# A one-core encoder layer in fp32: first tiles split by halves between the value weights, products of ones ahead of them, and the routing sums, tables and first two gathers in another order

## The chip, the cores and the metric

One of the cores of a Trainium2 chip runs the whole program; the other cores are idle. The time is that of one execution on the device, in microseconds (us). The kernel before takes 1265.24 us, the median of three runs (1263.52 to 1265.70). TensorE is called PE in the rows, VectorE DVE, ScalarE ACT, GpSimd POOL and SyncE SP; SP, ACT and POOL also issue transfers (DMAs).

## The reference, cut to what matters

Two requests (512 and 1024 tokens, 1536 together, 1024 features) go through one post-norm encoder layer with shared weights. Cut to its skeleton:

```python
proj = x @ w_in                        # queries, keys and values of two head groups
oa = windowed attention (+-128 tokens) with sinks and ALiBi
ob = dilated attention, three (window, dilation) branches merged by their denominators
x1 = LN(alpha * x + concat(rms(oa), rms(ob)) @ w_out)
scores = sigmoid(x1 @ w_router)        # 16 experts in 4 groups
# best group by the sum of its two best biased scores, then top 2 inside it
y = sum over the two experts of gate * (silu(x1 @ w_gate[e]) * (x1 @ w_up[e])) @ w_down[e]
shared = (silu(x1 @ ws_gate) * (x1 @ ws_up)) @ ws_down
out = LN(alpha * x1 + y + shared)
```

All values are fp32. The kernel makes each large product of three: every operand is split in a high part (ScalarE rounds it to the matmul type) and a low part (VectorE subtracts the high part from the original), and TensorE adds high by high, high by low and low by high.

## The kernel before, in words

Each engine has its own program, written out by hand in the order of its work; semaphores (`S[...]`) hold one engine until another has counted up. Nothing but this order and these waits schedules the work. The stages that the change touches:

**Value projection (the head, functions `xt`, `vpart`, `vproj`, lines 848 to 890).** SyncE loads token tile 0 into `xin` (L512), the identity (L513), tile 1 (L514) and then, for each of the 8 slices k of the input features, 512 and 128 columns of value weights into `raw_v` (L516, L517). TensorE waits for the identity, transposes tile 0 and tile 1 (8 transposes each, L852; the first eight lie in banks 0 and 1, the others in 2 and 3), ScalarE copies the high parts into `xT`, VectorE subtracts for the low parts (L1637). Only then do both go on to the value weights: `wv_hi` on ScalarE, `wv_lo` on VectorE (L1658), one slice after another. TensorE runs, for each k, the six products of tile 0 and the six of tile 1 (L858 to L860). Tiles 2 to 11 follow one by one, the transposes of tile t+1 ahead of the products of tile t. Meanwhile SyncE stores finished value tiles (`store_v`), loads the next token tile (`load_x`), and at t == 4 issues `load_small` (constants, router weights, sinks and gains, seven small transfers). GpSimd carries the rows of `w_out` through SBUF to a scratch copy in DRAM in split form (`wo_st` counts these stores).

**First keys and queries (`PRE` projections, `dup`).** Six projections of 24 products each (512 columns) go through one pair of stage buffers: ScalarE copies the high part (`proj_high`), VectorE the low part (`proj_low`), SyncE copies stage to `KA`, `KB` or `Q` (`dup`, L579, L583), and ScalarE may fill the stage again only when that copy has landed. Ahead of the first `dup` SyncE waits for all stores of `w_out` (`wo_st`, 32 * KD). After the five first copies it loads the next weights and writes zeros to the accumulator; the sixth copy opens `pair(0)`. In `pair` TensorE interleaves 72 attention units with projections.

**Shared expert and routing (`d_step`, `dgu`, `ddn`, `dxt`, lines 1045 to 1240).** A step works on 256 tokens: `dxt` transposes them, `dgu` makes 96 products with gate and up weights in four blocks f (0 and 1 are gate, 2 and 3 up), ScalarE takes Silu, VectorE multiplies by the up half (`gated`) and takes the low part (`h_low`), `ddn` makes 12 products with the down weights for each half of the tokens, and VectorE adds them to `base` (`add_shared`). The shared expert runs on the first three tiles (n = 0, 1, 2; `EARLY` is 3), then steps of 224 slots with routed experts follow, then three late steps of the shared expert. In VectorE's program the routing stands between: `route_scores` and `route_groups` (sigmoid, ranks, the mask `msk`), then TensorE's prefix sums over tokens (L1215, L1219, in bank 2, after `d_step(1)`), `route_slots` (the place of each token in its expert's run, about 35 small operations), three `route_tables(n)` (0/1 matrices `oneA` and `oneB`, all on VectorE), TensorE's `table(n)` (8 products each, L1205, between the `ddn` calls), and `route_done` (token ids, gates and destinations by slot). Its last instruction counts `table_ready`. GpSimd then copies two columns of ids (L2256), gathers the rows of slot tile 3 into `xg` (two indirect transfers, L2261), and TensorE transposes them. The gather of tile 4 waits until those transposes are done, since it writes the same `xg`.

**Expert weights.** SyncE loads gate and up weights of the next slot tile into `raw_gu` in two halves as soon as VectorE has split the half before (`wg_lo`), and the down weights into `raw_d` (`wd_lo`). The first of these loads waits for `ej_ready`, the list of experts from `route_slots`.

## Time and profile before

| | before |
|---|---|
| median of 3 runs | 1265.24 us |
| the profiled execution's own time | 1265.37 us |
| its span, first to last instruction | 1263.5 us |
| TensorE busy | 1204.5 us (95%) |
| VectorE busy | 734.5 us (58%) |
| ScalarE busy | 578.9 us (46%) |
| GpSimd busy | 214.5 us (17%) |
| mean granted TensorE clock | 0.98 |
| transfers, mean over the span | 188 GB/s |

The profile is of one execution. "Busy" counts the time in which an engine has an instruction at work; a wait of TensorE shows as idle time, and the row that ends it names what it waited for. The granted clock is 1.0 at the full of its two levels (2.4 GHz) and 0.5 at the lower (1.2 GHz). The span is 1.9 us shorter than the execution's own time.

### The profile page before, as it was taken

What the parts mean: (1) busy time and instruction counts of PE and PEld (TensorE: products, weight loads), DVE (VectorE), ACT (ScalarE), POOL (GpSimd) and SP (SyncE); (2) the same over time, 40 slices, a digit from 0 to 9 for tenths busy, and PEclk for the clock granted to TensorE, in tenths of its full rate; (3) what the DMA queues carried; (4) which work ended last, traced back from release to release, by engine and by line L of the source; (5) the groups of instructions that cost most, each with busy time, mean ns of one, the idle gap of its engine ahead of it and who ended that gap; (6) DMA issues with size and microseconds to landing.
All of it is one profiled execution on the core that took longest, in us unless ns stands there. A gap on an engine that the chain in (4) does not pass through costs nothing.

```text
span 1263.5 us, 22065 instructions
## 1 busy us (share of the span) xinstructions
PE 1204.5 (95%) x8031; PEld 1083.0 (86%) x8031; DVE 734.5 (58%) x1790; ACT 578.9 (46%) x1416; POOL 214.5 (17%) x276
## 2 busy tenths in 40 slices
PE   6999999999999999999799999998799999999993
PEld 6998788888888888888688888897799999999892
DVE  3222355655565556555767886458566656665378
ACT  3232244544454355434443343220466766666455
POOL 1021001200120012002211112000213333333222
PEclk9999999999999999999999999899899999999997
DMA  8697664356436543748763333532899999999783
GB/s 242 204 296 252 150 168 97 93 143 147 97 77 173 117 114 80 186 132 255 205 213 137 143 118 116 189 112 67 281 302 268 284 295 274 267 282 299 189 310 143
DMA packets 162802, 237.47 MB, mean 188 GB/s; under 512 B 41328, under 2 KB 111216, under 8 KB 162672
## 3 DMA queue, kind: packets, MB, share of 16 engines
q1 hardware_dynamic: 148400, 185.00, 48.8%
q0 software_dynamic: 11776, 41.95, 13.6%
q10 hardware_dynamic: 2544, 9.44, 1.9%
q8 instruction: 50, 0.82, 0.3%
q14 instruction: 32, 0.26, 0.1%
HBM read 147.44 MB, written 59.02 MB: 163 GB/s over the span
## 4 chain that ended last, share of the span: by engine, by line
PE 82%; issue 6%; DVE 4%; DMA 3%; ACT 2%; SPq 1%; POOL 1%; DVEq 1%; ACTq 0%; POOLq 0%
PE bank L858 18%; PE bank L860 18%; PE bank L859 18%; PE bank L959 9%; PE bank L852 5%; PE bank L946 5%; PE bank L937 4%; PE bank L938 3%; PE bank L1081 2%; SPq L579 1%; SPq L583 1%; DMA a_work<-in_x 1%; POOL Q L2211 1%; DMA wo_scratch<-a_work 1%; DMA d_work<-x_scratch,idc 1%
## 5 line engine op out<-in xcount | busy, mean ns | idle before, releaser
L1345 ACT ACTIVATE b_work<-b_work 128x256 f32<-128x256 f32 (+3 forms) x288 | 148.1, 514 | 235.3 <-DVE b_work L1691 235.2
L858 PE MATMUL bank<-xgT_hi,w_gu_hi 128*128 128x224 f32 (+1 forms) x704 | 197.5, 281 | 4.4 <-ACT d_work L1571 2.3
L859 PE MATMUL bank<-xgT_lo,w_gu_hi 128*128 128x224 f32 (+1 forms) x704 | 196.2, 279 | 0.0
L860 PE MATMUL bank<-xgT_hi,w_gu_lo 128*128 128x224 f32 (+1 forms) x704 | 196.1, 279 | 0.0
L1700 DVE COPY b_work<-bank 128x256 f32<-128x256 f32 (+2 forms) x256 | 112.8, 440 | 117.3 <-PE bank L946 116.3
L858 PEld LDWEIGHTS bank<-xgT_hi,w_gu_hi 128*128 128x128 f32 x704 | 136.6, 194 | 6.6 <-issue 3.1
L859 PEld LDWEIGHTS bank<-xgT_lo,w_gu_hi 128*128 128x128 f32 x704 | 136.7, 194 | 0.7
L860 PEld LDWEIGHTS bank<-xgT_hi,w_gu_lo 128*128 128x128 f32 x704 | 136.6, 194 | 0.0
L2211 POOL CAST Q<-Q 128x512 fp32r<-128x512 f32 x48 | 53.5, 1148 | 437.8 <-DVE w_k_lo L1645 232.0
L946 PE MATMUL bank<-keep,b_work 128*128 128x128 f32 x608 | 114.8, 275 | 7.0 <-ACT b_work L1345 6.8
L946 PEld LDWEIGHTS bank<-keep,b_work 128*128 128x128 f32 x608 | 79.8, 139 | 40.2 <-ACT b_work L1345 11.8
L959 PE MATMUL bank<-b_work 128*128 128x64 f32 (+1 forms) x704 | 107.4, 268 | 0.0
L959 PEld LDWEIGHTS bank<-b_work 128*128 128x128 f32 (+1 forms) x704 | 97.1, 193 | 7.5 <-issue 2.2
L1691 DVE CUSTOM_DVE_ANT_0 b_work<-bank,tB 128x256 f32<-128x256 f32 (+2 forms) x192 | 74.8, 390 | 44.3 <-PE bank L938 40.0
L1746 DVE TENSOR_TENSOR xgT_lo<-bank,xgT_hi 128x512 fp32r<-128x512 f32 (+1 forms) x88 | 52.3, 638 | 78.1 <-ACT xgT_hi L1253 78.1
L1455 ACT ACTIVATE w_gu_hi<-raw_gu 128x512 fp32r<-128x512 f32 (+1 forms) x144 | 77.6, 622 | 33.4 <-DVE c_work L1778 22.9
L1874 DVE TENSOR_TENSOR w_gu_lo<-raw_gu,w_gu_hi 128x512 fp32r<-128x512 f32 x136 | 83.3, 682 | 0.0
L858 PE MATMUL bank<-w_o,oT_hi 128*128 128x512 f32 x192 | 76.5, 398 | 1.8 <-DVE c_work L1760 1.2
L858 PE MATMUL bank<-xT,w_q_hi 128*128 128x512 f32 x192 | 77.2, 402 | 0.0
L1253 ACT ACTIVATE xgT_hi<-bank 128x512 fp32r<-128x512 f32 (+1 forms) x88 | 44.4, 558 | 71.4 <-PE bank L852 64.4
L860 PE MATMUL bank<-xT,w_q_lo 128*128 128x512 f32 x192 | 75.6, 394 | 0.0
L859 PE MATMUL bank<-xT,w_q_hi 128*128 128x512 f32 x192 | 75.4, 393 | 0.0
(214 smaller groups left out, 2835.5 us busy)
## 6 DMA issues: line engine op xcount, KB each, us to landing
raw_gu<-in_w_gate SPq DMA_DIRECT2D x32, 512.0 KB
raw_gu<-in_w_up SPq DMA_DIRECT2D x32, 512.0 KB
raw_d<-in_w_down SPq DMA_DIRECT2D x16, 1024.0 KB, 9.5
Q<-stage_hi SPq DMA_DIRECT2D x96, 128.0 KB, 2.4
Q<-stage_lo SPq DMA_DIRECT2D x96, 128.0 KB, 2.4
o_scratch<-b_work SPq DMA_DIRECT2D x36, 264.0 KB, 3.4
c_work<-o_scratch SPq DMA_DIRECT2D x12, 792.0 KB, 5.1
wo_scratch<-a_work POOLq DMA_DIRECT2D x16, 512.0 KB, 4.0
```

Of the source, the lines that this page charges most:

```text
L852: last = nc.tensor.transpose(banks[c // 4][:, P * (c % 4):P * (c % 4) + rows], src[0:rows, P * c:P * c + P], ident[0:rows, 0:rows])
L858: nc.tensor.matmul(o, w_hi, x_hi, start=first, stop=False)
L859: nc.tensor.matmul(o, w_hi, x_lo, start=False, stop=False)
L860: return nc.tensor.matmul(o, w_lo, x_hi, start=False, stop=last)
L946: end = nc.tensor.transpose(bank[2 + u % 2][0:r, P * c:P * c + P], prob[:, u % 2, at[c]:at[c] + r], ident)
L959: end = nc.tensor.matmul(o, probT[0:r, u % 2, P * c:P * c + P], rows, start=c == 0, stop=c == len(v) - 1)
L1345: nc.scalar.activation(prob[:, u % 2, 0:n], prob[:, u % 2, 0:n], ACT.Exp, scale=-1.0, bias=o[:, HD:HD + 1], accum_out=o[:, HD + 1:HD + 2])\
L1455: nc.scalar.activation(w[0][:, bass.ds(k * 512, 512)], raw_gu.rearrange("p k f -> p (k f)") [:, bass.ds(k * 512, 512)], ACT.Copy).then_inc ...
L1691: V.tensor_tensor_reduce(out=prob[:, u % 2, 0:n], in0=bank[u % 2][:, 0:n], in1=tab, scale=-(HD ** -0.5), scalar=BIG, op0=ALU.add, op1=ALU.min,
L1700: last = V.tensor_copy(probT[:, u % 2, 0:n], bank[2 + u % 2][:, 0:n])
L1874: V.tensor_tensor(w_lo[:, w], flat[:, w], plain(w_hi[:, w]), ALU.subtract)\
L2211: end = G.tensor_copy(to.rearrange("c (r s) -> c r s", r=4), plain(slot[:, half, part, :]).rearrange("c (s r) -> c r s", r=4))
```

## The change

In the head: SyncE loads the identity first, tile 0 second, and tile 1 behind the first slice of value weights. TensorE makes six products of ones into bank 7 before it waits for the identity. Tiles 0 and 1 are transposed with a count after each four (`xt_half`), and ScalarE and VectorE take their four quarters between the slices 0 and 1 of the value weights. The transposes of tile 2 go behind slice 5. The gains are loaded ahead of `load_x(4)`, the other small constants at t == 5, and SyncE's wait for `wo_st` moves from the first `dup` into `pair(0)`.

In the routing: VectorE takes `route_scores` ahead of `gated(0)`, `route_groups` behind it; the prefix sums go into `dgu(1)` behind block 2, in bank 7; the transposes of tile 2 go behind its blocks 0 and 1; both `ddn(0)` halves follow `dgu(1)`. In `route_slots` the expert list is cut out (`route_experts`, now after the first table), and the sums of the mask by score are woven in. `oneA` is made on ScalarE (`rows_hit`). The three `table(n)` stand in `dgu(2)` behind blocks 1 and 2 and after it. `route_done` makes the ids first and counts `id_ready`; GpSimd gathers tiles 3 and 4 at once, by the table's own columns, into `xg` and `slab`. The first expert's weights are split in two parts around `add_shared(1, 1, 1)`.

```diff
# SyncE
+            sp.dma_start(ident, const[:, 0:P]).then_inc(S["id_loaded"], 16)
             sp.dma_start(xin[:, 0, :], x_t[0]).then_inc(x_ld[0], 16)
-            sp.dma_start(ident, const[:, 0:P]).then_inc(S["id_loaded"], 16)
-            sp.dma_start(xin[:, 1, :], x_t[1]).then_inc(x_ld[1], 16)
             for k in range(KD):
+                if k == 1:
+                    sp.dma_start(xin[:, 1, :], x_t[1]).then_inc(x_ld[1], 16)
...
             load_w(KA0, KA0 + HD)
+            load_gains()
+            load_x(4)
             for t in range(4, TILES):
                 store_v(t - 4)
-                load_x(t)
-                if t == 4:
+                if t > 4:
+                    load_x(t)
+                if t == 5:
                     load_small()
...
-            sp.wait_ge(S["wo_st"], 32 * KD)
             for n in range(PRE - 1):
                 what, g = FIRST[n]
                 dup(n, what, g, g, KA)
...
+                if i == 0:
+                    sp.wait_ge(S["wo_st"], 32 * KD)
                 load_v1(i)
# TensorE, head
+            pe.wait_ge(S["ones_ready"], 1)
+            for c in range(6):
+                nc.tensor.matmul(bank[7][:, 0:P], ones, ones, start=True, stop=True)
             pe.wait_ge(S["id_loaded"], 16)
...
+            def xt_first(t):
+                pe.wait_ge(x_ld[t], 16)
+                for c in range(KD):
+                    made = nc.tensor.transpose(bank[2 * t + c // 4][:, P * (c % 4):P * (c % 4) + P],
+                                               xin[:, t, P * c:P * c + P], ident)
+                    if c % 4 == 3:
+                        made.then_inc(S["xt_made" if c > 4 else "xt_half"], 1)
...
-            xt(0)
-            xt(1)
-            pe.wait_ge(S["xts_ready"], 2)
+            xt_first(0)
+            xt_first(1)
             for k in range(KD):
                 pe.wait_ge(S["wv_made"], k + 1)
                 for t in range(2):
+                    if k == 0:
+                        pe.wait_ge(S["xts_half"], t + 1)
+                    if k == KD // 2:
+                        pe.wait_ge(S["xts_ready"], t + 1)
...
-            xt(2)
+                if k == 5:
+                    xt(2)
# ScalarE and VectorE, head (VectorE alike, with wv_low)
+            xt_part(0, 0)
+            wv_high(0)
+            xt_part(0, 1)
+            xt_part(1, 0)
+            wv_high(1)
+            xt_part(1, 1)
+            for k in range(2, KD):
+                wv_high(k)
+            xt(2)
# TensorE, routing
+            def second(f):
+                if f < 2:
+                    dxt(slab, f, 2, 2)
+                if f == 2:
+                    prefix_sums()
+
+            def third(f):
+                if f in (1, 2):
+                    table(f - 1)
+
+            dgu(1, 1, 1, second)
             pe.wait_ge(S["xg_lo"], 2 * EARLY)
...
-            dgu(2, 0, 2)
+            ddn(0, 0, 0, 0)
+            pe.wait_ge(S["cum_read"], 1)
+            ddn(0, 0, 1, 0)
+            dgu(2, 0, 2, third)
+            table(2)
             ddn(1, 1, 0, 1)
-            table(0)
             ddn(1, 1, 1, 1)
-            table(1)
-            table(2)
             ddn(2, 0, 0, 2)
-            ddn(2, 0, 1, 2)
             dxt(xg, 0, EARLY, EARLY)
             dxt(xg, 1, EARLY, EARLY)
+            ddn(2, 0, 1, 2)
# ScalarE, routing, at the head of d_step(2)
+            def rows_hit(n):
+                act.wait_ge(S["rq_ready"], 1)
+                if n == 2:
+                    act.wait_ge(S["idm_made"], 1)
+                a = oneA[:, n % 2].rearrange("p c a -> p (c a)")
+                for c in range(THIRD):
+                    nc.scalar.activation(a[:, P * c:P * c + P], iota_p, ACT.Square, scale=-1.0,
+                                         bias=rq[:, 0, THIRD * n + c:THIRD * n + c + 1])
+                act.drain()
+                nc.scalar.activation(a, plain(a), ACT.Relu, scale=-1.0, bias=1.0).then_inc(S["oneA_made"], 1)
# VectorE, routing, its order
+            route_scores()
             gated(0, 0, 0)
+            route_groups()
+            xg_low(2, 0, 2)
+            xg_low(2, 1, 2, bank[5:7])
             h_low(0, 0, 0)
-            route_scores()
-            route_groups()
+            route_slots()
             gated(1, 1, 1)
-            xg_low(2, 0, 2)
+            route_tables(0)
+            route_experts()
+            route_tables(1)
+            route_tables(2)
             h_low(1, 1, 1)
-            xg_low(2, 1, 2)
             add_shared(0, 0, 0)
-            route_slots()
-            route_tables(0)
+            route_done()
+            gated(2, 0, 2)
             add_shared(0, 0, 1)
-            gated(2, 0, 2)
-            route_tables(1)
             h_low(2, 0, 2)
-            route_tables(2)
             add_shared(1, 1, 0)
-            route_done()
+            gu_split(EARLY, 1, EARLY, range(0, 4))
             add_shared(1, 1, 1)
-            gu_split(EARLY, 1, EARLY)
+            gu_split(EARLY, 1, EARLY, range(4, KD))
+            xg_low(EARLY, 0, EARLY)
+            xg_low(EARLY, 1, EARLY, bank[0:2])
             add_shared(2, 2, 0)
             add_shared(2, 2, 1)
# GpSimd
+            def first_gathers():
+                pool.wait_ge(S["xgT_made"], 2 * EARLY)
+                pool.wait_ge(S["id_ready"], 1)
+                for n, (place, sems) in enumerate(((xg, ("g_first", "g_ld")), (slab, ("g_second", "g_second")))):
+                    for h in range(2):
+                        rows, c = half_rows(EARLY, h), 2 * n + h
+                        G.indirect_dma_start(out=place[0:rows, h, :], out_offset=None, in_=x1_d,
+                                             in_offset=bass.IndirectOffsetOnAxis(ap=idtab[0:rows, c:c + 1].bitcast(U32),
+                                                                                 axis=0)).then_inc(S[sems[h]], 16)
...
-            gather(EARLY)
-            gather(EARLY + 1)
+            first_gathers()
+            pool.wait_ge(S["table_ready"], 1)
             weights(EARLY)
             gather(EARLY + 2)
```

The sources and waits that follow from this are changed with it: step 3 takes tile 4 from `slab`, `y_rows` of step 3 waits until `slab` has been transposed, and the next gather (tile 5) waits only for the transposes of tile 3.

## Rows read from the trace of the kernel before

**Rows 1.** Profile page, busy time of TensorE: us, share of the span, instructions.

```profile
PE 1204.5 (95%) x8031; PEld 1083.0 (86%) x8031; DVE 734.5 (58%) x1790; ACT 578.9 (46%) x1416; POOL 214.5 (17%) x276
```

**Rows 2.** Stretches: us, busy (instructions) of PE, PEld, DVE, ACT, POOL; clock, DMA share, GB/s.

```profile
4.61:8.30 3.69, 3.67 (x16) 3.16 (x16) 0.57 (x1) 1.09 (x2) 0.00 (x0) 1.00 1.04 374
14.87:27.39 12.52, 12.52 (x86) 12.52 (x85) 1.73 (x3) 0.69 (x3) 3.36 (x6) 0.99 0.79 175
833.87:868.00 34.13, 34.13 (x260) 32.76 (x261) 25.34 (x84) 4.20 (x8) 0.00 (x0) 1.00 0.18 60
868.00:898.76 30.76, 19.95 (x88) 16.21 (x86) 24.46 (x44) 8.54 (x17) 4.28 (x5) 0.78 0.40 123
892.30:902.50 10.20, 6.98 (x33) 6.69 (x34) 6.01 (x11) 6.11 (x12) 2.73 (x4) 0.50 1.02 344
914.00:932.00 18.00, 18.00 (x138) 16.52 (x139) 11.75 (x20) 10.96 (x21) 1.57 (x3) 1.00 0.98 347
```

**Rows 3.** Timeline of the head: start, us, engine, line, instruction, [idle before <- releaser].

```profile
1.15 0.42 SPq L513 DMA_DIRECT2D keep<-in_const  x1
10.64 5.96 DVE L1658 TENSOR_TENSOR w_v_lo<-a_work,w_v_hi 128x640 fp32r<-128x640 f32 x8
11.60 0.59 PE L858 MATMUL bank<-w_v_hi,xT 128*128 128x384 f32 x1 [3.32 <-DVE w_v_lo L1658]
30.92 0.44 PE L858 MATMUL bank<-w_v_hi,xT 128*128 128x384 f32 x1 [1.62 <-DVE xT L1637]
46.63 1.09 PE L852 MATMUL bank<-keep,a_work 128*128 128x128 f32 x8 [0.48 <-DMA a_work<-in_x]
```

**Rows 4.** Timeline of the first keys and queries, 116 to 163 us.

```profile
116.01 0.60 ACT L1253 ACTIVATE stage_hi<-bank 128x512 fp32r<-128x512 f32 x1 [4.62 <-PE bank L860]
120.20 0.52 SPq L579 DMA_DIRECT2D KA<-stage_hi  x1
144.47 0.35 PE L937 MATMUL bank<-KA,Q 128*128 128x256 f32 x1 [1.00 <-DMA Q<-stage_lo]
153.40 0.60 ACT L1253 ACTIVATE stage_hi<-bank 128x512 fp32r<-128x512 f32 x1 [2.40 <-issue]
160.87 0.60 ACT L1253 ACTIVATE stage_hi<-bank 128x512 fp32r<-128x512 f32 x1 [2.67 <-DMA KB<-stage_lo]
163.04 0.33 PE L946 MATMUL bank<-keep,b_work 128*128 128x128 f32 x1 [1.87 <-ACT b_work L1345]
```

**Rows 5.** Timeline of the routing on all engines, 835 to 894 us.

```profile
835.77 0.16 DVE L1965 COPY r_work<-keep 128x24 f32<-128x24 f32 x1
845.38 0.36 DVE L1985 SCALAR_TENSOR_TENSOR r_work<-r_work 128x192 f32<-128x192 f32 x1
856.22 0.28 DVE L2002 TENSOR_TENSOR r_work<-bank,r_work 128x112 f32<-128x112 f32 x1 [2.41 <-PE bank L1219]
865.18 0.19 DVE L2060 CAST r_work<-rq_i 128x48 f32<-128x48 int32 x1
880.21 2.01 PE L1205 MATMUL bank<-oneB,oneA 128*128 128x180 f32 x8 [3.23 <-DVE oneB L2084]
884.33 1.59 POOL L2261 DMA_INDIRECT d_work<-x_scratch,idc  x1 [0.92 <-POOL idc L2256]
893.37 3.25 PE L852 MATMUL bank<-keep,d_work 128*128 128x128 f32 x16 [4.02 <-DMA d_work<-x_scratch,idc]
```

**Rows 6.** What the moved comparison costs: VectorE's group, and ScalarE's scaled and plain copies.

```profile
L2080 DVE TENSOR_TENSOR oneA<-r_work,keep 128x1024 fp32r<-128x1024 f32 x3 | 3.7, 1219 | 0.0
46.73 0.28 ACT L1253 ACTIVATE Va<-bank 128x128 f32<-128x128 f32 x1
46.89 1.34 ACT L1296 ACTIVATE a_work<-a_work,keep 128x512 fp32r<-128x512 f32 x2
```

**Rows 7.** An expert's gate and up weights: issue of a load, and its splitting on ScalarE.

```profile
921.01 0.38 SPq L741 DMA_DIRECT2D raw_gu<-in_w_gate  x1
935.30 4.27 ACT L1455 ACTIVATE w_gu_hi<-raw_gu 128x512 fp32r<-128x512 f32 x8
```

More of the change, by code:

```diff
@@ L1044, in dxt @@
                     transposes(src[:, half, :], bank[0:2], S["xgT_made"], R1)
+                    return
+                if n == 2 and half:
+                    transposes(src[:, half, :], bank[5:7], S["xgT_made"])
                     return
@@ L1534, in d_step @@
                 soon = n in (0, EARLY, LATE0, LATE0 + 1)
+                if n == EARLY - 1:
+                    for third in range(3):
+                        rows_hit(third)
                 if EARLY <= n - 2 < LATE0 - 1:
@@ L1571, in d_step @@
                 nc.scalar.activation(hidden(sg[:, s, :], n), hidden(bank[0][:], n), ACT.Silu).then_inc(S["sg_ready"], 1)
-                if not last and not soon and n != EARLY - 1:
+                if not last and not soon and n >= EARLY:
                     xg_high(q + 1, 0, n + 1)
@@ L1579, in d_step @@
                     xg_high(q + 1, 1, n + 1, bank[0:2])
-                elif not last and not soon:
+                elif not last and not soon and n >= EARLY:
                     xg_high(q + 1, 1, n + 1)
@@ L1652, in proj_low, with xt_part, wv_low @@
                 V.tensor_tensor(lo, sums, plain(hi), ALU.subtract).then_inc(S["proj_ready"], 1)
-            xt(0)
-            xt(1)
-            for k in range(KD):
+            def xt_part(t, c):
+                dve.wait_ge(S["xs_hi" if c else "xs_half"], t + 1)
+                hi, lo = (xT[:, 0, part, 4 * c:4 * c + 4, P * t:P * t + P] for part in range(2))
+                V.tensor_tensor(lo, bank[2 * t + c][:].rearrange("p (k c) -> p k c", c=P), plain(hi), ALU.subtract)\
+                 .then_inc(S["xts_ready" if c else "xts_half"], 1)
+            def wv_low(k):
                 dve.wait_ge(S["wv_hi"], k + 1)
@@ L1659, in _ @@
                                 plain(wv_hi[:, 640 * k:640 * k + 640]), ALU.subtract).then_inc(S["wv_made"], 1)
+            xt_part(0, 0)
+            wv_low(0)
+            xt_part(0, 1)
+            xt_part(1, 0)
+            wv_low(1)
+            xt_part(1, 1)
+            for k in range(2, KD):
+                wv_low(k)
             def wo_low(k):
```

121 lines of the change are left out of this document (66 added, 55 removed).

## The prediction, made before the changed kernel ran

> **What bounds the kernel now.** The page's busy times come first: TensorE works 1204.5 us, 95% of the span [rows 1]. So only two things can shorten the time: a gap of TensorE that closes, or products at the full clock that ran at the lower one. I therefore went through TensorE's timeline stage by stage and wrote down every gap with the row that ends it; the views by stretch then give the sum and the clock. In the routing, from 868.00 to the first expert step at 898.76, TensorE is busy 19.95 of 30.76 us at a mean clock of 0.78, while the 34.13 us before are full at 1.00 [rows 2]. The largest gaps there are 3.23 us for a table of VectorE's and 4.02 us for gathered rows [rows 5]. In the head it waits 3.32 us for the value weights' low part, 1.62 us for tile 2 and 0.48 us for a tile's load [rows 3]. Around the first attention units it waits 1.00 us for a copy to Q and 1.87 us for ScalarE, which a copy to KB holds [rows 4]. In the expert steps it is full: 18.00 of 18.00 us at clock 1.00 [rows 2]. What is won ahead of them should thus stay won, if the weight stream follows.
>
> **The head, step by step.** Identity and tile 0 change places, 576 KB in both orders, and TensorE started at 4.61 when the second had landed [rows 2, 3]. I keep 4.6. The 16 first transposes took 3.67 us, 0.23 each, against 1.09 us for eight later ones, 0.13 each [rows 2, 3]: they ran at the lower clock, although the stretch's own row prints 1.00. Tile 0 costs 8 x 0.23 = 1.84 us, to 6.45. Tile 1 now stands behind 320 KB of weights, at 374 GB/s 0.9 us; it had some half us in hand, so I charge 0.4. Its transposes end at 6.85 + 1.84 = 8.7.
>
> The weights' first low part is no longer behind four quarters: half of tile 0 is transposed at 5.5, ScalarE's copy and VectorE's part take about 0.6 us each and the slice's copy and part 0.65 and 0.75 (5.96 / 8, [rows 3]), so it is made at about 7.5 to 8. The slices after it come every 0.75 us, TensorE takes 1.75 for one. Products start at 8.7 rather than 11.60. The 96 products take 96 x 12.52 / 86 = 14.0 us at full clock [rows 2]; I add 0.4 for a start at the lower one. Two sets of transposes at 0.87 net follow (tile 2 inside the loop, tile 3 after it). Tile 2's products start at 8.7 + 14.0 + 0.4 + 1.7 = 24.8 instead of 30.92 [rows 3]: **6.1**. The wait of 1.62 goes with it, since tile 2 is converted under slices 6 and 7. The 0.48 for a load goes too, as the small constants no longer stand ahead of it: **0.5**.
>
> The products of ones are an operation that the trace does not show by itself. At 0.23 each they are 1.4 us, over long before the first load lands: cost 0. If they raise the clock by 4.6, the transposes gain up to 16 x 0.10 = 1.6 us. A loss would need a later start, and nothing is behind them until 4.6. I take 0, because a pause of 2 us lies between, and keep 1.6 for the range.
>
> The first `dup` waited for the stores of w_out until 120.20, while its stage was filled at 116.01 + 0.6 + 0.7 = 117.3 [rows 4]. With that wait gone the chain of copies starts 2.9 us earlier still, and TensorE's gap of 1.00 closes: **1.0**. ScalarE's waits of 2.40 and 2.67 for the same copies shrink by about 2, so the 1.87 at 163.04 closes: **1.9**. The moved wait is harmless: SyncE reaches it some 30 us after the stores are done. Behind it stand `load_v1` and `load_v2`, first needed at unit 24. The head sums to **9.5**.
>
> **The routing, step by step.** I set one timetable, in the times of the trace before, from dgu(1) at 833.87.
>
> VectorE: scores move from 835.77 to 832.7, behind the low part of tile 1. They take 5.8 us, `gated(0)` 0.6 (to 839.1), groups 4.2 (the whole from 835.77 to 845.38 + 0.4 is 10.0 [rows 5]): the mask is ready at 843.2. TensorE: 260 products in 34.13 us are 0.13 each [rows 2], a block of 24 (256 columns) 2.9 us, eight transposes 0.87; blocks 0 to 2 with both transposes end at 844.4, so there is 1.1 in hand. The sums (3.3 us) end at 847.6. `gated(0)` would hold block 2 from 841.5; 2.4 in hand.
>
> `route_slots` took 865.18 + 0.19 - 856.22 = 9.15 us to the rows and columns [rows 5]. The expert list takes 1.3 away, the woven sums bring 0.8: 8.65, to 856.3, then 0.8 for the gates, `gated(1)` to 857.8. TensorE meanwhile has block 3 (850.6), two `ddn` of 2.9 (856.4) and dgu(2), whose table(0) stands at 862.3. VectorE's first table takes 2.5 us, to 860.3: 2 in hand.
>
> ScalarE makes `oneA` from 858.4 on. The trace has no Square of 128 columns with a pointer. The plain copy of 128 is 0.28; two scaled of 512 take 1.34, about 0.18 more than two plain ones, a pointer is 0.09; overlapped by 0.09, one is 0.28 [rows 6]. Eight are 2.25, the Relu over 1024 about 1.05, a drain 0.2: 3.5 us a third. The ends for the range are 1.22, VectorE's own price for the same 1024 columns [rows 6], and 8 x 0.67 + 1.3 = 6.7, were each as long as 512 columns. The thirds are ready at 861.9, 865.4 and 868.9, and TensorE wants them at 862.3, 866.1 and 869.9. So in hand are only 0.4, 0.7 and 1.0. The row says that ScalarE takes three times VectorE's 1.22 for this work. The Trainium skill (ScalarE: Activation LUTs, Rules for kernel authors) says the same as a rule: relu and other simple elementwise work belongs on VectorE. By the rule the comparison would stay there: VectorE's last table would be 3 x 1.14 later, at 870.7, and TensorE would wait 0.8. By the rows ScalarE is idle here (8.54 busy in 30.76 us, [rows 2]), so I cost the slower engine at 0.
>
> TensorE ends the last table at 870.8 and runs ddn(1, 0), ddn(1, 1), ddn(2, 0) to 879.4. The ids are ready at 871.2. The first gather was issued at 884.33 and both had landed by 893.37, 9.0 us, with 2 MB of weights beside them [rows 5]. Now 0.9 us of id copying is gone. At 9.0 the rows of tile 3 land at 880.4 and cost 1 us; alone, perhaps 7.5 and nothing. Their transposes end at 881.0, the last ddn at 883.9, the low parts at 884.2. The first expert step starts at 884.3 instead of 898.76: **14.5**. Checked from the other side: 10.8 us of gaps plus half of some 8.5 us of busy time at the lower clock are 15.0. Then that step ran at the lower clock until 902.50, where the stretch prints 0.50 [rows 2]: half of 3.7 is **1.9**. The routing sums to **16.4**.
>
> **What follows it.** The first expert's load begins no earlier (`ej_ready` moves from 859.4 to 861.9), but the next begins only 8.4 us earlier while its use is 14.5 earlier. ScalarE's three stores of `base` (3 MB) move forward as well. In the steady part a load is issued at 921.01 and split from 935.30, 14.3 us, with the transfer engines 98% busy at 347 GB/s [rows 2, 7]. The loads of tiles 5 and 6 get about 11 us. ScalarE may run some 3 us late before its Silu is late: I charge 0, and this is the likeliest place for a loss.
>
> **The sum.** 9.5 + 16.4 = 25.9, less 0.5 for the places with under 1 us in hand: 25.4. The profiled execution took 1265.37, within 0.15 of the median 1265.24, so **1240.0**.
>
> **The rivals.** (a) The weight stream or the gathers give some back. For it: the 98% and the eleven us; against it: no expert step of before waits for a weight. 2 to 7 us: 1242 to 1247. (b) The head gives less, because tile 1 or the value weights arrive later than the even 374 GB/s says, or the lower clock lasts: products from 10.5 and 1.6 more, 3.4 us: 1243.5. (c) The tables turn: ScalarE at 6.7 a third pushes the three tables by about 3, 6 and 9 us, and ids with them. 9 us: 1249. A table load between Silu and Square would cost only 1.3 once. The Trainium skill (ScalarE: Activation LUTs, Table sets) says that cheap functions such as relu stand in every set, which speaks against such a load; the trace shows no Square right behind a Silu in this stage. (d) The stream, not TensorE, sets the pace of the experts, so that they end when they did and the whole routing gain is swallowed: 1256. (e) Slower than before: the 14.3 us become the bound. ScalarE splits the weights ahead of its Silu, so a load landing late holds Silu, `gated`, the split of the hidden values and ddn in each of about 15 routed steps. It decides from 25.4 / 15 = 1.7 us a step; at 2 us a step 1265.4 - 25.4 + 30 = 1270. Against it: the steps are as long as before and ask for the same bytes, so a late start should be made up. (f) It does not do what it says: VectorE's own order costs TensorE what the table's waits cost, and only the head is left: 1256 as in (d).
>
> **How the numbers follow.** Forecast, everything within 1237 to 1242: 0.56. (a) 0.20, (b) 0.10, (c) 0.05, (d) and (f) 0.05, (e) 0.03, a gain above the forecast by the 1.6 of the ones 0.01. Low: 1240 - 1.6 - 1.4 for waits that I charged, 1237. High: through (a) and (b), 1248; beyond it lie (c) to (e), 0.13. About 0.2%, 2.5 us, is what a measurement can tell from no change. Faster: all but (e) and a remainder, 0.96; same 0.01; slower 0.03.
>
> **What would show it.** Tile 2's products at 24 to 26 us instead of 30.92; no wait for Q at the first unit and none of 1.87 behind it; from dgu(1) to the first expert step some 50.5 us with under 2 of gaps and a clock of 1.00; table products that wait for nothing or under 1 us for `oneA`; transposes of tile 3 at about 9 us behind the ids. Wrong would be: a wait for raw_gu on ScalarE with TensorE gaps behind 890, a first table behind 863, or value products that start later than 10.

## The result, and the profile after

The changed kernel took 1245.5 us (median of 4 runs, 1241.7 to 1247.8) beside 1265.5 of the kernel before: a ratio of 0.983, 95% interval 0.981 to 0.985, so it is 20 us faster. Forecast were 1240.0, with 1237 to 1248. Side and range hold; the sum was 5.5 us too good, and the result lies outside the band of 1237 to 1242 that the forecast proper gave 0.56, in that of the rivals (a) and (b). The execution profiled is the slowest of the four, 1247.77 us (span 1245.9).

The page's busy times of the changed kernel:

```profile
PE 1200.8 (96%) x8043; PEld 1079.9 (87%) x8043; DVE 730.3 (59%) x1787; ACT 589.1 (47%) x1443; POOL 217.2 (17%) x274
```

TensorE is busy for 3.7 us less than in [rows 1], with 12 more instructions, and the span is 17.6 us shorter: 13.9 us of the gain are closed gaps, the rest is busy time. The same stretches as in [rows 2] (us, busy of PE, PEld, DVE, ACT, POOL, granted clock, DMA share, GB/s), and one of the attention:

```profile
14.87:25.50 10.63, 10.63 (x77) 10.63 (x76) 2.74 (x4) 2.12 (x6) 3.35 (x6) 1.00 1.08 230
157.60:164.40 6.80, 6.45 (x23) 5.88 (x24) 3.02 (x10) 1.99 (x8) 0.00 (x0) 0.50 0.96 267
832.12:866.25 34.13, 33.98 (x261) 32.82 (x262) 28.12 (x88) 13.27 (x34) 0.00 (x0) 1.00 0.12 33
866.25:881.71 15.46, 15.46 (x88) 12.75 (x87) 14.28 (x29) 8.12 (x15) 4.43 (x4) 1.00 0.82 232
```

From the second shared block's start (832.12, before 833.87) to the first expert step (881.71, before 898.76) TensorE now runs 49.44 of 49.6 us, all at the full clock. These 49.6 were 64.9. The stretch at 157.60 ran at 0.50, the lower level; the kernel before was at 1.00 there.

The head's timeline, to be held against [rows 3]:

```profile
1.03 2.93 PE L874 MATMUL bank<-keep 128*128 128x128 f32 x12 [1.03 <-DVE keep L1705]
4.95 1.06 PE L880 MATMUL bank<-keep,a_work 128*128 128x128 f32 x8 [0.99 <-DMA a_work<-in_x]
8.08 1.97 PE L880 MATMUL bank<-keep,a_work 128*128 128x128 f32 x8 [2.07 <-DMA a_work<-in_x]
9.70 0.67 PE L866 MATMUL bank<-w_v_hi,xT 128*128 128x384 f32 x1
...
26.13 0.42 PE L866 MATMUL bank<-w_v_hi,xT 128*128 128x384 f32 x1
```

The six fp32 products of ones are 12 instructions in 2.93 us. Tile 0's eight transposes took 1.06 us, the pace of the full clock; tile 1's took 1.97 after 2.07 us of waiting for its load. Tile 2's products start at 26.13 instead of 30.92. The first keys and queries, against [rows 4]:

```profile
110.46 0.60 ACT L1298 ACTIVATE stage_hi<-bank 128x512 fp32r<-128x512 f32 x1 [4.62 <-PE bank L868]
111.81 0.51 SPq L581 DMA_DIRECT2D KA<-stage_hi  x1
119.93 0.60 ACT L1298 ACTIVATE stage_hi<-bank 128x512 fp32r<-128x512 f32 x1 [8.88 <-DMA KA<-stage_lo]
139.06 0.36 PE L962 MATMUL bank<-KA,Q 128*128 128x256 f32 x1 [0.97 <-DMA Q<-stage_lo]
155.77 0.60 ACT L1298 ACTIVATE stage_hi<-bank 128x512 fp32r<-128x512 f32 x1 [2.99 <-DMA KB<-stage_lo]
157.95 0.69 PE L971 MATMUL bank<-keep,b_work 128*128 128x128 f32 x2 [2.19 <-ACT b_work L1405]
```

The copy to KA is issued at 111.81, 8.4 us earlier than before, but ScalarE can use the stage again only at 119.93. The gaps of 1.00 and 1.87 that I expected closed are there: 0.97 and 2.19. The routing, against [rows 5, 6]:

```profile
830.09 1.28 ACT L1651 ACT_TABLE_LOAD   x1
856.61 2.44 ACT L1600 ACTIVATE oneA<-keep,r_work 128x128 fp32r<-128x128 f32 x8
859.11 1.06 ACT L1603 ACTIVATE oneA<-oneA 128x1024 fp32r<-128x1024 f32 x1
860.23 1.13 PE L1252 MATMUL bank<-oneB,oneA 128*128 128x180 f32 x8
868.92 0.22 DVE L2184 TENSOR_SCALAR idtab<-bank 128x60 int32<-128x60 f32 x1 [1.09 <-PE bank L1252]
870.06 1.10 POOL L2353 DMA_INDIRECT d_work<-x_scratch,idtab  x1 [63.78 <-DVE idtab L2184]
877.24 1.78 PE L860 MATMUL bank<-keep,d_work 128*128 128x128 f32 x16
884.47 2.19 ACT L1515 ACTIVATE w_gu_hi<-raw_gu 128x512 fp32r<-128x512 f32 x4 [4.30 <-DMA raw_gu<-in_w_up]
892.05 0.85 PE L860 MATMUL bank<-keep,slab 96*128 96x96 f32 x8 [1.17 <-DVE xgT_lo L1841]
```

A third of `oneA` takes 2.44 + 1.06 = 3.5 us; it ends at 860.17, and the table's products start at 860.23 without a wait. The gathered rows are transposed 8.1 us behind the end of the ids' row (869.14), without a wait, but with nothing in hand: in e5, whose trace has the landings, the second half lands at 874.63 and its transposes start at 874.80. One small new wait, 1.17 us, stands in the second expert step. It comes from the weights: ScalarE waits 4.30 us for a load, so VectorE's low parts of the weights and, behind them, of the rows come late. That is the sign that the prediction had named for being wrong, a wait for `raw_gu` with a gap of TensorE's behind 890.

The profiled execution, added up: 5.5 us gained by the first key projection (104.7 for 110.3), 3.8 lost again by the second shared block (832.12 for 833.87 is all that is left), 15.3 gained to the first expert step, 0.5 behind it: 17.6. Of the 3.8, 2.3 go ahead of the first shared block (787.7 for 790.9) and 1.5 between it and the second, where this stretch was at the lower clock:

```profile
806.10:816.30 10.20, 10.04 (x47) 10.08 (x48) 5.07 (x6) 3.24 (x8) 0.18 (x1) 0.50 1.01 396
```

Every profile has such a stretch there. It lasts 6.8 us in eight of them (before, e1, e2, e4 to e7, e12; 42.9 to 43.0 us from block to block) and 10.2 us in six (the first of the changed kernel, e3, e8 to e11; 44.3 to 44.5 us). The changed kernel had 10.2 in its first profile and 6.8 in e5, so this 1.5 us differs between executions of one program; whether the change makes the longer one likelier isn't shown.

### The profile page after: what moved, and what is told of

Same layout as the page of the kernel before. It is cut to its first block, busy times and chain, and to the rows that moved or that the text cites. A ratio compares the mean times of both kernels' runs of the same rounds, so it can differ in the third digit from the quotient of the medians.

```text
span 1245.9 us, 22130 instructions
## 1 busy us (share of the span) xinstructions
PE 1200.8 (96%) x8043; PEld 1079.9 (87%) x8043; DVE 730.3 (59%) x1787; ACT 589.1 (47%) x1443; POOL 217.2 (17%) x274
## 4 chain that ended last, share of the span: by engine, by line
PE 75%; issue 10%; DVE 4%; DMA 3%; ACT 2%; POOL 2%; SPq 2%; ACTq 1%; POOLq 0%; DVEq 0%
PE bank L866 17%; PE bank L868 16%; PE bank L867 16%; PE bank L984 9%; PE bank L971 5%; PE bank L860 4%; PE bank L962 4%; PE bank L963 3%; SPq L585 1%; POOL c_work L2278 1%; PE bank L1114 1%; DMA KA<-stage_lo 1%; DVE c_work L1873 1%; SPq L581 1%; DVE c_work L1871 1%
## 5 line engine op out<-in xcount | busy, mean ns | idle before, releaser
L868 PE MATMUL bank<-w_o,oT_lo 128*128 128x512 f32 x192 | 74.9, 390 | 0.0
```

The lines of the kernel that those rows point to most:

```text
L868: return nc.tensor.matmul(o, w_lo, x_hi, start=False, stop=last)
```

## The experiments

Each was timed in five rounds beside the kernel before; "gain" is one less the ratio, with its 95% interval, in us of 1266. Times of different jobs are compared by these ratios.

**One half at a time.** The head's edits alone (e1), then the routing's alone (e2).

> The kernel before with the head's half of the change alone. My theory after reading the changed kernel's profile: the head brings 5.5 us by the start of the first key projection (104.7 instead of 110.3 us) and nothing more, because the copies into Q arrive no earlier and the wait of 1.87 us behind the first units stays. So 1265.4 - 5.5 = 1259.9 us if TensorE's clock falls as often as before; rival: the earlier head also makes the clock fall once more near 158 us (cost about 3.4 us), so 1263 us, and the profile then shows a stretch at the lower clock between 150 and 170 us. The prediction as put down would say 1255.9.

> The kernel before with the routing's half of the change alone. The changed kernel's profile shows 49.6 us from the second shared block's products to the first expert step instead of 64.9, and one new wait of 1.2 us in the second expert step. So 1265.4 - 15.3 - 1.9 (no lower clock behind the routing) + 1.2 = 1249.4 us. Rival: the gain is partly given back in the expert steps by the weight stream, so 1252 or more, with waits for raw_gu. The prediction as put down would say 1249.0.

e1: 1262.6 against 1267.5, ratio 0.9958 (0.9945 to 0.9972), gain 5.3 us (3.5 to 7.0). e2: 1250.0, ratio 0.9865 (0.985 to 0.988), gain 17.1 us (15 to 19). Together 22.4, the change 21.6. The prediction had 9.5 and 16.4: the routing's sum stands, the head's is what failed. The profile of e2 from the second shared block to the first expert step:

```profile
833.72:883.24 49.52, 49.36 (x346) 45.59 (x346) 42.32 (x116) 21.38 (x48) 4.42 (x4) 1.00 0.33 100
```

It is 49.5 us, as in the changed kernel; the routing's gain doesn't hang on the head. In e1 the first key projection starts at 106.0 instead of 110.3, and the stage is free 8.9 us behind its filling (9.2 in the kernel before).

**The wait for w_out's stores put back** (e3):

```diff
+            sp.wait_ge(S["wo_st"], 32 * KD)
             for n in range(PRE - 1):
                 what, g = FIRST[n]
                 dup(n, what, g, g, KA)
@@ pair(0)
-                if i == 0:
-                    sp.wait_ge(S["wo_st"], 32 * KD)
```

> The changed kernel with the wait for w_out's stores put back ahead of the first copy to KA. Theory: the copies' landing is set by what stands ahead of them in the transfer queues, not by that wait, so the changed kernel's time, 1245.5, within 1 us, and the first copy to KA is issued later than 111.8 us but lands within 1 us of 119.9. Rival (the prediction as put down): removing the wait brought up to 2.9 us, so 1248 us, with the gap for Q growing from 0.97 to 2 or more.

1243.2 us, ratio 0.9812 (0.9798 to 0.9827); the changed kernel had 0.9829 and, in another job (e5), 0.9826. The wait costs nothing that can be measured. Its timeline:

```profile
110.92 0.60 ACT L1297 ACTIVATE stage_hi<-bank 128x512 fp32r<-128x512 f32 x1 [4.62 <-PE bank L867]
114.74 0.51 SPq L581 DMA_DIRECT2D KA<-stage_hi  x1
119.08 0.60 ACT L1297 ACTIVATE stage_hi<-bank 128x512 fp32r<-128x512 f32 x1 [7.56 <-DMA KA<-stage_lo]
```

Issued 2.9 us later, the copy was done 0.85 earlier: 8.2 us from filling to free stage, against 9.5 in the first profile and 8.3 to 9.5 in all eight in which the copy is issued at once and the tables stand ahead of it. An earlier issue brings nothing. The gap for Q was gone here; it is 0.97 in the first profile of the changed kernel, 0.79 in e5 and 0.27 in e7, so one profile doesn't show much about it.

**What stands ahead of the copies.** In e4 the 1 MB of zeros is stored behind the first value loads instead of ahead of the copy to KB. In e8 the three rotation tables, besides, are loaded behind the first copy to KA.

```diff
@@ e4 and e8
-            sp.wait_ge(S["zeros_ready"], 1)
-            for h in range(2):
-                sp.dma_start(acc_d[TOKENS + P * h: ...
@@ pair(0), behind load_v2(0)
+                    sp.wait_ge(S["zeros_ready"], 1)
+                    for h in range(2):
+                        sp.dma_start(acc_d[TOKENS + P * h: ...
@@ e8: the same five lines, now behind dup(0)
-            for s in range(2):
-                sp.wait_ge(vb_st[s], 48 * (TILES // 2) + 16)
-            sp.dma_start(tA, ...   and t1, t2
             for n in range(PRE - 1):
                 dup(n, what, g, g, KA)
+                if n == 0:
+                    ...
```

> The changed kernel with the 1 MB of zeros for the spare accumulator rows stored behind the first loads of values instead of ahead of the first copy to KB. Theory: that copy takes 5.1 us from its issue instead of the usual 2.4 because the zeros and a weight load stand ahead of it; moved, it lands about 2 us earlier, TensorE's wait of 2.19 us at 155.8 us closes, and with it the fall of the clock at 157.6 to 164.4 us (3.4 us). So 1245.5 - 2.2 = 1243.3 us, and down to 1240 if the fall is always there in the changed kernel and is set off by that wait. Rival: the weight load of 512 KB alone delays the copy, the wait stays above 1.5 us, and the time stays at 1245.5.

> The changed kernel with the zeros stored behind the first value loads (as in the run before this) and, besides, the loads of the three rotation tables moved from ahead of the first copy to KA to behind it. Theory: that copy waits in the transfer queues behind the tables (three loads) and a weight load; it lands 1 to 2 us earlier than 119.3, each copy behind it follows, and TensorE's wait for Q at 138 us (0.87) closes, so 0.9 us less than with the zeros alone: 1240.7. Rival: the weight load and the stores of w_out are what holds it, it lands at 119 as before, and the tables, now later, hold the first bias and rotation steps on VectorE: the same or up to 1 us more than 1241.6.

e4: 1241.6 us, ratio 0.9797 (0.9784 to 0.981). e8: 1241.6, ratio 0.9803 (0.978 to 0.9825). Both are 0.2 to 0.3% better than the changed kernel in the middle of their intervals; e4's interval lies below that of the first measurement, e8's overlaps e5's, and between e4 and e8 no difference was measured. First e4's timeline, then e8's:

```profile
154.16 0.60 ACT L1299 ACTIVATE stage_hi<-bank 128x512 fp32r<-128x512 f32 x1 [0.49 <-DMA KB<-stage_lo]
```

```profile
110.87 0.60 ACT L1300 ACTIVATE stage_hi<-bank 128x512 fp32r<-128x512 f32 x1 [4.62 <-PE bank L870]
117.16 0.60 ACT L1300 ACTIVATE stage_hi<-bank 128x512 fp32r<-128x512 f32 x1 [5.70 <-DMA KA<-stage_lo]
139.57 0.44 PE L973 MATMUL bank<-keep,b_work 128*128 128x128 f32 x2 [0.96 <-ACT b_work L1407]
151.55 0.60 ACT L1300 ACTIVATE stage_hi<-bank 128x512 fp32r<-128x512 f32 x1 [0.48 <-DMA KB<-stage_lo]
```

With the zeros gone ScalarE waits 0.49 instead of 2.99 us for the copy to KB, and TensorE's 2.19 behind it closes; the wait for Q stays, at 0.87. With the tables gone too, the stage is free 6.3 us after its filling instead of 9.5, and the wait for Q closes. In e4 not all of this is the zeros' doing: TensorE was at the lower clock for 3.4 us from 140.6, came later to the place where it waits for ScalarE, and so waited less. Four profiles with such a stretch and the zeros where they were (e5, e7, e9, e10) have 0.57, under 0.3, 0.67 and 0.34 us there. e8 has no such stretch, and the wait is closed all the same, against 1.74 to 2.65 us in the profiles without one (e1, e6).

A measure that is free of this is the time from the first key projection to the first shared block. It is 680.7 and 679.3 us with the old head (before, e2), 678.5 to 683.0, on the mean 680.5, in the eight profiles with the new head and the loads unmoved, and 676.8 in e8: some 3.5 us for the two moves, and nothing for the change itself. e8 reaches the first shared block at 781.9 us, against 790.8 in the kernel before: 9.0 us, nearly what the prediction promised of the head (9.5), by other edits.

**The same two moves in the kernel before** (e12), nothing of the change in it:

> The kernel before, with nothing of the change, but with the two moves behind the first attention units: tables behind the first copy to KA, zeros behind the first value loads; its wait for w_out's stores stays. Theory: the terms of 1.0 and 1.9 us that the prediction ascribed to that wait belong to what stands ahead of the copies in the transfer queues. So TensorE's gaps of 1.00 at 143 and 1.87 at 163 us close here too, although the wait stands: 1266.4 - 2.9 = 1263.5. Rival: in the kernel before the wait is what holds the first copy (issued at 120.20), and the gap for Q stays at 0.5 us or more.

1262.4 us, ratio 0.997 (0.9956 to 0.9985), gain 3.8 us (1.9 to 5.6). The timeline:

```profile
118.85 0.52 SPq L579 DMA_DIRECT2D KA<-stage_hi  x1
124.05 0.60 ACT L1255 ACTIVATE stage_hi<-bank 128x512 fp32r<-128x512 f32 x1 [7.23 <-DMA KA<-stage_lo]
143.30 0.36 PE L939 MATMUL bank<-KA,Q 128*128 128x256 f32 x1
160.56 0.44 PE L948 MATMUL bank<-keep,b_work 128*128 128x128 f32 x2 [0.57 <-ACT b_work L1347]
```

Its wait for w_out's stores stands, and yet the 1.00 for Q is gone and the 1.87 is 0.57. From the first key projection to the first shared block it takes 677.1 us, 2.9 less than the mean of before and e2. So the 2.9 us were to be had without taking the wait out. But the theory holds only in part. The first copy is issued at 118.85 instead of 120.20 and the stage is free 5.2 us behind that, where it was 5.0: the copy itself is no faster, and the wait still holds it, 1.3 us behind the filled stage. The wait is over sooner, probably because w_out's stores no longer share the transfer engines with the tables. The waits for Q and ScalarE are also smaller by chance at times: e2, with this same start and neither move, has 0.41 and 1.40.

**The start.** e6 loads tile 1 ahead of the first value slice; e7 leaves the six products of ones out (they enter no result).

```diff
@@ e6
+            sp.dma_start(xin[:, 1, :], x_t[1]).then_inc(x_ld[1], 16)
             for k in range(KD):
-                if k == 1:
-                    sp.dma_start(xin[:, 1, :], x_t[1]).then_inc(x_ld[1], 16)
@@ e7
-            pe.wait_ge(S["ones_ready"], 1)
-            for c in range(6):
-                nc.tensor.matmul(bank[7][:, 0:P], ones, ones, start=True, stop=True)
```

> The changed kernel with the load of tile 1 ahead of the first slice of the value weights. Theory: in the changed kernel the products start at 9.70 us because tile 1's load lands at 8.08, while the first slice's low part is made at 7.7 already; so tile 1 lands 0.9 to 1.3 us earlier, the products start at about 8.8 and the time falls by 0.9 us, which the times alone will hardly show, the start of the products will. Rival: the first slice, now second, becomes the bound: its low part at 9 or later, and the products start no earlier than 9.5.

> The changed kernel without the six products of ones. Theory: the first eight transposes, 1.07 us in the changed kernel, take 1.9 to 2.0 us again, and nothing else moves, because tile 1's load sets when the products start (9.7 us): the time stays within 0.3 us. Rival: the products of ones raise the clock for the first value products too; without them tile 1's transposes stay at 1.97 and the first 20 us of products take up to 1.6 us longer, so the products of tile 2 start at 27 us or later instead of 26.1.

e6: 1244.1 us, ratio 0.983 (0.9803 to 0.9857). e7: 1244.6, ratio 0.9825 (0.9801 to 0.9848). Neither differs from the changed kernel's 0.9826 (e5) in the same job. e6's timeline, then e7's:

```profile
5.04 3.65 PE L879 MATMUL bank<-keep,a_work 128*128 128x128 f32 x16 [1.09 <-DMA a_work<-in_x]
9.07 0.45 PE L865 MATMUL bank<-w_v_hi,xT 128*128 128x384 f32 x1 [0.39 <-DVE w_v_lo L1743]
```

```profile
5.00 1.94 PE L877 MATMUL bank<-keep,a_work 128*128 128x128 f32 x8 [5.00 <-DMA a_work<-in_x]
8.61 1.97 PE L877 MATMUL bank<-keep,a_work 128*128 128x128 f32 x8 [1.67 <-DMA a_work<-in_x]
```

TensorE no longer waits for tile 1; it waits 0.39 us for the low part of the weights, and the products start at 9.07. By the first key projection the move counts for more: 103.8 and 103.9 us (e6, e11) against 104.7 to 106.3, mean 105.4, in the nine other profiles with the new head. Without the ones the eight transposes took 1.94 us. But with the ones, too, they took the fast pace in only four executions (first, e3, e4, e11) and the slow one in six. Without them it was slow in all four (before, e2, e7, e12), so the ones probably raise the clock at times; and the 0.9 us is lost in the wait for tile 1 in any case, for tile 2's products start at 26.84 us in e7 and at 26.98 in e5, which has the ones.

**The changed kernel once more** (e5), beside e6 to e8:

> The changed kernel once more, beside its variants, as their common measure. By the first measurement 1245.5 us against 1265.5 before, a ratio of 0.983. One more profile of it shows which gaps and which stretches at the lower clock return: theory: the gap for Q (0.97 us at 138 us) and the one of 2.19 us at 155.8 us are there again within 0.3 us, while the fall of the clock at 157.6 may come or not, and the spread of the runs of one kernel (6 us) is that of the time spent at the lower clock. Rival: the fall at 157.6 is always there and is part of what the change costs.

1245.0 us, ratio 0.9826 (0.9802 to 0.9849). The wait for Q is 0.79; that of ScalarE's copy came out at 1.38 and TensorE's gap at 0.57 instead of 2.19; the clock fell at 141.8, not at 157.6. The two belong together: the 3.4 us at the lower clock let TensorE come later to its wait for ScalarE, and the gap there shrinks by 1.6. New in it is a wait that the first profile doesn't have. Its timeline at 904 us, then the stretch behind it:

```profile
904.15 2.19 ACT L1515 ACTIVATE w_gu_hi<-raw_gu 128x512 fp32r<-128x512 f32 x4 [6.22 <-DMA raw_gu<-in_w_up]
904.81 2.50 DVE L1969 TENSOR_TENSOR w_gu_lo<-raw_gu,w_gu_hi 128x512 fp32r<-128x512 f32 x4 [5.58 <-ACT w_gu_hi L1515]
907.78 1.29 DVE L1841 TENSOR_TENSOR xgT_lo<-bank,xgT_hi 128x512 fp32r<-128x512 f32 x2
...
909.21 0.97 PE L860 MATMUL bank<-keep,d_work 96*128 96x96 f32 x8 [1.98 <-DVE xgT_lo L1841]
```

```profile
909.80:913.20 3.40, 3.40 (x12) 2.35 (x10) 1.02 (x2) 2.03 (x4) 1.83 (x3) 0.50 0.90 275
```

The second half of the third expert tile's weights lands late, ScalarE splits it 6.2 us late, VectorE's low part of the weights stands ahead of the low part of the rows, and TensorE waits 1.98 us for that. Then it ran at 0.50 for a stretch. All executions with the new routing, by ScalarE's wait for these weights and TensorE's behind it:

| | e10 | e2 | e3 | e8 | first | e4 | e9 | e5 | e7 | e11 | e6 |
|---|---|---|---|---|---|---|---|---|---|---|---|
| ScalarE, us | 0 | 1.26 | 2.03 | 2.81 | 3.79 | 5.11 | 5.50 | 6.22 | 6.29 | 7.37 | 7.57 |
| TensorE, us | 0 | 0 | 0 | 0 | 0 | 0.88 | 1.27 | 1.98 | 2.07 | 3.14 | 3.34 |

ScalarE has 4.2 us in hand, and what goes beyond reaches TensorE one to one; the mean is 1.2 us. In the kernel before ScalarE splits all eight parts at 917.03 without a wait.

**The cover of the routing.** e9 makes `oneA` on VectorE again, inside the tables; e10 puts the 16 transposes of the first gathered rows behind the last down products.

```diff
@@ e9, rows_hit is gone
+                V.tensor_tensor(a, rq[:, 0, c].unsqueeze(2).to_broadcast([P, THIRD, P]),
+                                iota_p.unsqueeze(1).to_broadcast([P, THIRD, P]), ALU.is_equal)\
+                 .then_inc(S["oneA_made"], 1)
@@ e10
+            ddn(2, 0, 1, 2)
             dxt(xg, 0, EARLY, EARLY)
             dxt(xg, 1, EARLY, EARLY)
-            ddn(2, 0, 1, 2)
```

> The changed kernel with the comparison that makes the rows' one-hot factor back on VectorE, in the tables, as in the kernel before; ScalarE's eight squares and one relu a third are gone. By the changed kernel's profile the first table is then made at 859.6 instead of 858.5, the second at 865.5 and the third at 869.3; TensorE wants them at 860.23, 864.09 and 867.86. Theory: TensorE waits about 1.4 us in all for the tables (1.4 for the second, the third then in time within 0.1), the first expert step starts 1.4 us later behind the second shared block's start (51.0 instead of 49.6), and the time is up to 1.4 us longer. The prediction had 0.8. Rival: the change of engine brought nothing, the gathers and not the tables set the end, and the first expert step starts 49.6 us behind as before.

> The changed kernel with the 16 transposes of the first gathered rows behind the last down products of the shared block instead of ahead of them. Theory: these 3.0 us of products are the only cover of the copies and low parts behind the transposes (3.2 us from the first copy to the last low part). Without it TensorE waits about 2 us ahead of the first expert step, so 51.6 instead of 49.6 us from the second shared block to it, and the time is 2 us longer: 1247. Rival: the first low parts are enough to start, the wait is under 0.8 us.

e9: 1246.5 us, ratio 0.9843 (0.9816 to 0.9869). e10: 1249.2, ratio 0.9855 (0.9829 to 0.988). From the second shared block to the first expert step e9 needs 52.7 us and e10 52.4, instead of 49.6. e9's timeline, then e10's:

```profile
864.68 1.10 PE L1252 MATMUL bank<-oneB,oneA 128*128 128x180 f32 x8 [1.84 <-DVE oneB L2177]
```

```profile
883.08 0.37 PE L866 MATMUL bank<-xgT_hi,w_gu_hi 128*128 128x224 f32 x1 [2.76 <-DVE xgT_lo L1841]
```

The waits are 1.84 (expected 1.4) and 2.76 (expected 2), and behind each the clock was at the lower level for a stretch (866.4 to 869.8; 883.8 to 887.2); e9's is the rest of its 3.1 us, e10's comes on top of its 2.8. By the profiles both covers are real. The times agree in direction, some 2 us for e9 and 3.5 for e10 by the middles of the ratios, but the intervals of both overlap the changed kernel's.

**All three moves of loads together** (e11, the edits of e6 and e8):

> The changed kernel with all three moves of loads together: tile 1 ahead of the first value slice, the tables behind the first copy to KA, the zeros behind the first value loads. Theory: the gains add in the profile, as they lie at different waits: products from 9.1 us (0.6 earlier), no wait for Q at 138 and none of ScalarE's at 155, the first shared block at about 781 (787.6 in the changed kernel, 781.9 with the two later loads alone). Times 1240.6, that is 4.3 less than the changed kernel's 1245. Rival: the copies' pace, 5.5 us each, takes back the earlier start, and it is 1241.6 as without tile 1's move.

1239.8 us, ratio 0.9785 (0.9761 to 0.9809): the best kernel of the study, 0.4% below the changed one in the middle of the intervals; it overlaps e5's a little and the first measurement's not at all. Its stage is free at 115.90, nothing waits for Q, and the first shared block starts at 780.6, 10.2 us ahead of the kernel before. Its profiled execution, with 3.14 us of waiting for the late weights, was the slowest of its six (1244.3).

## Why the prediction was right, and where it was wrong

**Head, 6.1 + 0.5: right in kind, 1.1 too large.** Tile 2's products came at 26.13, not 24.8 (26.98 in e5). The step that failed is tile 1's load, "I charge 0.4": it landed at 8.08, not 6.85, and at 7.99 to 8.96 in the nine profiles with this order. I spread 374 GB/s evenly, a figure of [rows 2] from a stretch in full flow, and took the loads to land in their order. In the time up to tile 1's landing the transfers moved less, first before, then changed:

```profile
2.00:8.08 6.08, 3.48 (x16) 3.17 (x16) 0.35 (x1) 1.47 (x3) 0.00 (x0) 1.00 0.97 344
```

```profile
2.00:8.08 6.08, 3.02 (x18) 2.52 (x17) 1.83 (x3) 2.10 (x4) 0.00 (x0) 0.95 0.92 306
```

By an estimate from the stretches of the changed kernel, 1.9 MB had moved by 8.08, while tile 1 and all that stands ahead of it are 1.44 MB: the weight slices issued behind tile 1 took their share too. The half microsecond that I gave tile 1 in hand was no safe figure either: in e2, with the old order, it landed at 7.74 and TensorE waited 1.21 us for it. This is rival (b) in part.

**The copies, 1.0 + 1.9: wrong.** The step: "With that wait gone the chain of copies starts 2.9 us earlier still". The copy is issued earlier and lands no earlier than with the wait (e3). I took the time from issue to landing as fixed. The trace of before shows why it isn't, in stretches that I hadn't read: between the filled stage (117.3) and the issue at 120.20 [rows 4] the transfer engines are full, and only then do they empty.

```profile
117.30:120.20 2.90, 2.90 (x15) 2.39 (x14) 0.03 (x1) 0.00 (x0) 0.00 (x0) 1.00 0.98 377
120.20:125.24 5.04, 5.04 (x24) 4.18 (x23) 0.00 (x0) 0.00 (x0) 0.00 (x0) 1.00 0.60 154
```

In the changed kernel the copies enter while they are full, at a share of 1.00 until 117, and move with the rest; the last of the copy then comes 2.9 us later, at a share of 0.14, and what holds this remainder isn't shown:

```profile
111.80:117.00 5.20, 5.20 (x24) 4.30 (x24) 0.00 (x0) 0.00 (x0) 0.00 (x0) 1.00 1.00 334
117.00:119.90 2.90, 2.90 (x14) 2.39 (x14) 0.00 (x0) 0.00 (x0) 0.00 (x0) 1.00 0.14 40
```

That the moved wait is harmless holds: no gap of TensorE's stands behind it in its new place, and in its old one it cost nothing measurable (e3). What held the copies in the changed kernel was shown by moving it away: the tables those to KA, the zeros that to KB (e8).

**The ones: 0 was right**, since the wait for tile 1 takes any gain (e7).

**The lower clock in the attention: a term I didn't have, and it costs little.** In 7 of the 11 profiles with the new head there is a stretch at the lower clock between 140 and 165 us, 3.4 us long each and 6.8 in the first; in the 3 with the old head there is none, and none in e1, e6, e8 and e11. That the waits there cause it isn't shown: e1, e6, before and e2 have the waits and no fall. By itself such a stretch would cost up to 1.7 us, or 3.4. But where it stands ahead of the wait for the copy to KB it takes the place of that wait. From the first key projection to the first shared block the six profiles with a fall and unmoved loads take 680.4 us on the mean, and the four without one (before, e1, e2, e6) 680.4 as well.

**Routing, 14.5 + 1.9: the 14.5 right, the 1.9 not on the mean.** 15.3 in the profile; the routing alone gained 17.1 us by its times (e2). Behind the first expert step e2's profile is 1.4 us shorter than before's, the first of the changed kernel 0.5, and the mean of the eleven (365.1 us) no shorter than the three with the old routing (364.7 to 364.9): the late weights below, with the lower clock behind them in some, take most of it back. The timetable held part by part: `oneA` 3.5 a third, 0.1 us in hand at the first table (0.4 forecast), transposes 8.1 behind the ids (9.0). I had costed the slower engine at 0 because it is idle, and e9 bears that out: on VectorE the same comparison delays the second table by 1.84 us. The rule against it, relu and simple elementwise work on VectorE (the Trainium skill, ScalarE: Activation LUTs, Rules for kernel authors), would have cost 3.1 us here by e9's profile, where the prediction had 0.8; the measurement decides. No table load came between Silu, Square and Relu, the one at 830.09 being Silu's own; for Relu that fits the Trainium skill (ScalarE: Activation LUTs, Table sets), by which cheap functions such as relu stand in every set. Square isn't named there among the cheap ones; for it the trace alone speaks.

**The weight stream, 0: rival (a) came true in small.** I had called it the likeliest place for a loss and given it 2 to 7 us; in the third expert step it is 1.2 on the mean, and some clock behind it, and in the first profile 1.17 in the second. Whether the three early stores of `base` or the rest of the traffic delay these weights wasn't tried.

The first profile's span is 17.6 us shorter where the sum had 25.4. By its stretches:

| us gained | forecast | first profile |
|---|---|---|
| to the first key projection | 6.6 | 5.5 |
| from there to the first shared block | 2.9 | -2.3 |
| to the second shared block | 0 | -1.5 |
| to the first expert step | 14.5 | 15.3 |
| behind it | 1.9 | 0.5 |
| set aside | -0.5 | |

So most of what is missing lies in the copies' term. The execution profiled is the slowest of the four, and its -2.3 and -1.5 are at the bad end: over the eight profiles with the new head and unmoved loads the second row is -0.5 on the mean, still 3.4 short of 2.9. The times are 5.5 us short, less than this profile. The range held by luck in part: its upper end came from rivals (a) and (b), and neither has the copies' term in it, where most is missing.

## What to carry to other kernels

Taking out a wait ahead of a transfer is worth something only if the transfer then lands earlier: read how full the transfer engines are at the moment to which you want to pull the issue, and if they are full, move what stands ahead of the transfer. Don't judge a gap by itself: a stretch at the lower clock ahead of it can take its place, so compare the time between two fixed points, over several profiles. When a stage is pulled forward by 15 us, the first loads behind it lose their slack, and it takes several profiles to see a wait that only half of the executions have. An idle engine three times slower can be the right place for work, if the timetable shows it ready in time.

## What the hardware did that I had not expected

A gap of TensorE can cost more than its length: the gaps of 1.84 (e9), 1.98 (e5), 2.76 (e10), 3.14 (e11) and 3.34 us (e6) between 860 and 910 us had a stretch of 3.4 us at the lower clock behind them or at their end, worth some 1.5 us more; that of 2.07 (e7) had none. It is no rule of this case: of the five gaps of 1.74 to 2.65 us at about 158 us (163 in the kernel before) two had such a stretch, in the first profile and in e3, and three had none, in e1, e6 and before. The same program differs in this from one execution to the next. The runs of the changed kernel go with the mean granted clock, 1241.7 us at 0.988 and 1247.8 at 0.985; these 0.003 of the span are 3.7 us, so they don't account for all of the 6.1.
